# Up runs with the activations stationary, and chunks of u, m and h turned by VectorE and through memory

## What is computed

```
xn = rmsnorm(x);  proj = xn @ w_in
y_mla = mla_branch(proj) @ w_mla_branch;  y_fox = fox_branch(proj) @ w_fox_branch
h  = x + (g_mla * y_mla + g_fox * y_fox) @ w_out        # m is the bracket
hn = rmsnorm(h, mlp_norm)
u  = square(relu(hn @ w_up))                            # 2048 -> 8192
h  = h + u @ w_down                                     # 8192 -> 2048
out = rmsnorm(h, final_norm)
```

## Time and profile before

| | |
|---|---|
| median of three executions | 1311.14 us (1311.02 to 1311.55) |
| the profiled execution, its own time | 1311.39 us |
| its span in the profile | 1309.6 us |
| mean granted clock of TensorE | 0.998 |
| PE busy | 99% of the span |
| DVE / ACT / POOL busy | 57% / 47% / 2% |
| moved by DMA | 251.36 MB, mean 192 GB/s |

### The profile page before, as it was taken

How to read it: one execution, slowest core, us unless ns; L and a number is a source line. 1 busy time by engine, 2 the same in 40 slices (tenths; PEclk the granted TensorE clock), 3 DMA queues, 4 the chain that set the end, 5 groups by cost and what they waited for, 6 DMA issues and landing times.

```text
span 1309.6 us, 15786 instructions
## 1 busy us (share of the span) xinstructions
PE 1300.0 (99%) x6504; PEld 1101.7 (84%) x6504; DVE 751.1 (57%) x803; ACT 609.5 (47%) x744; POOL 22.2 (2%) x20
## 2 busy tenths in 40 slices
PE   9999999999999999999999999999999999999997
PEld 8888888888888888888888888888888888888886
DVE  6676566545666566555666664444456666544543
ACT  6645444545445444454444443333344444444443
POOL 0100000000220000000000000000000000000000
PEclk9999999999999999999999999999999999999999
DMA  8656655556665475566566666666666666666663
GB/s 329 239 186 211 202 165 171 189 168 192 193 193 154 133 241 178 191 189 176 188 189 188 187 190 199 194 193 193 194 185 187 187 187 192 227 191 200 190 194 124
DMA packets 68840, 251.36 MB, mean 192 GB/s; under 512 B 7832, under 2 KB 7840, under 8 KB 68128
## 3 DMA queue, kind: packets, MB, share of 16 engines
q1 hardware_dynamic: 67104, 243.04, 59.8%
q0 software_dynamic: 656, 5.26, 1.1%
q10 hardware_dynamic: 1008, 2.05, 0.4%
HBM read 248.21 MB, written 2.11 MB: 191 GB/s over the span
## 4 chain that ended last, share of the span: by engine, by line
PE 99%; DMA 0%; DVE 0%; ACT 0%; SPq 0%; DVEq 0%; issue 0%; ACTq 0%
PE bank L505 26%; PE bank L585 19%; PE bank L586 19%; PE bank L587 19%; PE bank L510 13%; PE bank L683 1%; PE bank L659 1%; DMA raw<-weights 0%; PE bank L647 0%; PE bank L633 0%; PE bank L631 0%; PE bank L634 0%; PE bank L661 0%; DVE hl L1038 0%; ACT hl L818 0%; PE bank L490 0%
## 5 line engine op out<-in xcount | busy, mean ns | idle before, releaser
L1038 DVE TENSOR_TENSOR hl<-raw,hl 128x1024 fp32r<-128x1024 f32 x455 | 560.5, 1236 | 486.0 <-ACT hl L818 481.1
L818 ACT ACTIVATE hl<-raw 128x1024 fp32r<-128x1024 f32 x455 | 479.5, 1058 | 551.3 <-PE bank L587 383.0
L505 PE MATMUL bank<-hn_hl,hl 128*128 128x512 f32 x1024 | 321.7, 395 | 0.0
L510 PEld LDWEIGHTS bank<-hn_hl,hl 128*128 128x128 f32 x1024 | 192.4, 188 | 45.4
L510 PE MATMUL bank<-hn_hl,hl 128*128 128x256 f32 x1024 | 201.2, 278 | 0.0
L585 PE MATMUL bank<-hl,u_hl 128*128 128x512 f32 x512 | 199.2, 389 | 0.0
L586 PE MATMUL bank<-hl,u_hl 128*128 128x512 f32 x512 | 199.2, 389 | 0.0
L587 PE MATMUL bank<-hl,u_hl 128*128 128x512 f32 x512 | 199.2, 389 | 0.0
L505 PEld LDWEIGHTS bank<-hn_hl,hl 128*128 128x128 f32 x1024 | 156.0, 189 | 0.3
L585 PE MATMUL bank<-hl,x_hl 128*128 128x512 f32 x320 | 125.8, 393 | 0.0
L587 PE MATMUL bank<-hl,x_hl 128*128 128x512 f32 x320 | 124.7, 390 | 0.0
(11 more groups left out here) (180 smaller groups left out, 995.4 us busy)
## 6 DMA issues: line engine op xcount, KB each, us to landing
raw<-weights SPq DMA_DIRECT2D x455, 512.0 KB, 4.2
x_rows<-x_n POOLq DMA_DIRECT2D x2, 1024.0 KB, 10.3
resid<-x_n POOLq DMA_DIRECT2D x1, 2048.0 KB, 8.5
x_in<-x_t SPq DMA_DIRECT2D x3, 512.0 KB, 8.0
cum_k<-cum_rows POOLq DMA_DIRECT2D x1, 1024.0 KB, 7.3
gain_rows<-final_gain SPq DMA_DIRECT2D x1, 1024.0 KB, 4.2
out_n<-final SPq DMA_DIRECT2D x4, 256.0 KB, 2.9
out_n<-final ACTq DMA_DIRECT2D x4, 256.0 KB, 2.8
```

Source lines behind the costliest of these rows:

```text
L505: nc.tensor.matmul(ps, hl[:, slot, 0, col:col + P], x.rearrange("p h t -> p (h t)"), start=first, stop=False)
L510: return nc.tensor.matmul(ps[:, T:], hl[:, slot, 1, col:col + P], x[:, 0], start=False, stop=end)
L818: nc.scalar.activation(hl[:, slot, 0], raw[:, slot], ACT.Copy).then_inc(unit_hi, 1)
L1038: nc.vector.tensor_tensor(hl[:, slot, 1], raw[:, slot], hl[:, slot, 0].bitcast(F32), ALU.subtract).then_inc(unit_split, 1)
```

## The change

Up becomes TOKEN work: `FF_CHUNKS`, eight groups of 8 units for each part, in place of sixteen groups of 4. Its results have tokens on the partitions now, so u has to be turned as well. All chunks of u (16), and the first three chunks each of m and h, 22 in all, are turned in a new way: DVE transposes 32x32 blocks in place of PE's 128x128 (`turn_blocks`, into `blocks`); GpSimd stores `blocks`, 128x1024 float32, to `turn_rows` in memory with one transfer, waits for it, and reads it back with four transfers of 32 partitions each, 4 times 256 elements for a partition, into `turned`. Then ACT and DVE make the high and low part from `turned`. This comes six units (`TURN_UNITS`) after the group's own results are taken. The fourth chunk of m and of h is still turned by PE. The square of the positive part becomes ACT's Relu from PSUM and a multiplication by the bank on DVE. For h the gain is multiplied in by DVE beforehand, in two instructions, in place of ACT's scale.

```diff
@@ the groups @@
-            add(f"up{part}", g, FEATURE, KT // SLABS)
+        for g in range(FF_CHUNKS):
+            add(f"up{part}", g, TOKEN, KT // WIDE_SLABS)
...
-TURN_M = [BY["y_mla", g + 1].u0 + 1 for g in range(3)] + [BY["w_out", 0].u0 + 2]
-TURN_H = [BY["w_out", g + 1].u0 + 3 for g in range(3)] + [BY["up0", 0].u0 + 1]
+TURNED = [("y_mla", g) for g in range(CHUNKS - 1)] + [("w_out", g) for g in range(CHUNKS - 1)]
+TURNED += [(f"up{part}", g) for part in range(MLP_PARTS) for g in range(FF_CHUNKS)]
+TURN_NO = {key: n for n, key in enumerate(TURNED)}
+TURN_UNITS = 6
+TURN_M = BY["w_out", 0].u0 + 2
+TURN_H = BY["up0", 0].u0 + 2
...
+        if (gr.name, gr.g) in TURN_NO:
+            what = {"y_mla": "m turned", "w_out": "h turned"}.get(gr.name, "u turned")
+            after(gr.last + TURN_UNITS, what, gr.g if gr.name[:2] != "up" else gr)
...
@@ GpSimd @@
+            for n in range(len(TURNED)):
+                pool.wait_ge(blocks_turned, n + 1)
+                pool.dma_start(turn_rows[n % 2], blocks[:]).then_inc(blocks_stored, 16)
+                pool.wait_ge(blocks_stored, 16 * (n + 1))
+                if n:
+                    pool.wait_ge(turned_in, 4 * 16 * n)
+                if n >= 2:
+                    pool.wait_ge(turned_split, n - 1)
+                for q in range(4):
+                    pool.dma_start(turned[32 * q:32 * q + 32, n % 2].rearrange("p (a e) -> p a e", a=4),
+                                   turn_rows[n % 2, :, T * q:T * q + T].rearrange("(a p) e -> p a e", a=4)
+                                   ).then_inc(turned_in, 16)
...
@@ TensorE @@
-                token_units(gr, o_mla, last=2)
-                turn_m(g - 1)
-                token_units(gr, o_mla, first=2)
+                token_group(BY["y_mla", g], o_mla)
...
-                token_units(gr, m_hl, last=4)
-                turn_h(g - 1)
-                token_units(gr, m_hl, first=4)
+                token_group(BY["w_out", g], m_hl)
...
-                    else:
-                        feature_units(gr, hn_hl)
+                    else:
+                        token_units(gr, hn_hl)
...
+                def hidden_ready(i, up=up):
+                    pe.wait_ge(turned_split, TURN_NO[up, i // 2] + 1)
...
@@ ScalarE @@
+            def positive_part(gr):
+                act.wait_ge(unit_used, gr.last + 1)
+                act.wait_ge(blocks_turned, TURN_NO[gr.name, gr.g])
+                nc.scalar.activation(full[:], bank[:, gr.pair:gr.pair + 2], ACT.Relu).then_inc(positive, 1)
...
+                n = TURN_NO[gr.name, gr.g]
+                act.wait_ge(turned_in, 4 * 16 * (n + 1))
+                nc.scalar.activation(tiles_of(u_hl, 4 * gr.g, 0), turned_chunk(n), ACT.Copy).then_inc(u_hi, 1)
...
@@ VectorE @@
+            def turn_blocks(name, g, tile):
+                n = TURN_NO[name, g]
+                if n:
+                    dve.wait_ge(blocks_stored, 16 * n)
+                nc.vector.transpose(blocks[:].rearrange("p (q k b j) -> p k b q j", q=4, k=4, b=TB),
+                                    tile.rearrange("p b (k q j) -> p k b q j", k=4, q=4)).then_inc(blocks_turned, 1)
+            def turned_to_lo(n, tile, k0):
+                nc.vector.tensor_tensor(tiles_of(tile, k0, 1), turned_chunk(n), tiles_of(tile, k0, 0).bitcast(F32),
+                                        ALU.subtract).then_inc(turned_split, 1)
...
+                elif gr.name in HIDDEN0:
+                    dve.wait_ge(positive, HIDDEN0[gr.name] + gr.g + 1)
+                    nc.vector.tensor_tensor(full[:], full[:], both, ALU.mult).then_inc(token_out, 1)
+                    dve.wait_ge(token_out, gr.n + 1)
+                    turn_blocks(gr.name, gr.g, full[:])
...
+                    for n_b in range(TB):
+                        ins = nc.vector.tensor_tensor(
+                            turned_chunk(n)[:, :, n_b], turned_chunk(n)[:, :, n_b],
+                            gains.unsqueeze(2).unsqueeze(3).broadcast_to([P, 4, 4, 32]), ALU.mult)
+                    ins.then_inc(h_gained, 1)
```

More of the change, by code:

```diff
@@ L123 @@
 BY = {(gr.name, gr.g): gr for gr in GROUPS}
+RESID0 = {"w_out": 0, "down0": CHUNKS, "down1": 2 * CHUNKS}
 def number_groups():
@@ L164, in make_due @@
                 after(middle, "scored", pair + 1)
[L165 to L171, removed]
+        if (gr.name, gr.g) in TURN_NO:
+            what = {"y_mla": "m turned", "w_out": "h turned"}.get(gr.name, "u turned")
+            after(gr.last + TURN_UNITS, what, gr.g if gr.name[:2] != "up" else gr)
+        if gr.name == "w_out" and gr.g == 0:
+            after(TURN_M, "m turned", CHUNKS - 1)
         elif gr.name == "up0" and gr.g == 0:
-            after(middle - 1, "h turned", 3)
+            after(TURN_H, "h turned", CHUNKS - 1)
         if gr is GROUPS[-1]:
@@ L389, in program @@
         SPLIT0 = {Q_NORM: 0, KV_NORM: KQ}
-        FULL0 = {"up0": 0, "up1": FF_GROUPS}
-        RESID0 = {"w_out": 0, "down0": CHUNKS, "down1": 2 * CHUNKS}
+        HIDDEN0 = {"up0": 0, "up1": FF_CHUNKS}
         FROM_X = ("krff", "fq", "fk")
@@ L952, in take @@
                         nc.scalar.activation(std_col[:, MLP_NORM, 0:1], cst[:, C_EPS:C_EPS + 1], ACT.Sqrt)
-                elif gr.name in ("up0", "up1"):
-                    hidden_hi(gr)
+                elif gr.name in HIDDEN0:
+                    positive_part(gr)
             def m_to_hi(g):
[L957 to L961, removed]
-            def h_to_hi(g):
[L964 to L968, removed]
-                                         scale=gain[:, G_MLP + k:G_MLP + k + 1]).then_inc(h_hi, 1)
+                if g < CHUNKS - 1:
+                    n = TURN_NO["y_mla", g]
+                    act.wait_ge(turned_in, 4 * 16 * (n + 1))
+                    nc.scalar.activation(tiles_of(m_hl, 4 * g, 0), turned_chunk(n), ACT.Copy).then_inc(m_hi, 1)
+                else:
+                    act.wait_ge(m_turned, 1)
+                    nc.scalar.activation(m_hl[:, 4 * g:4 * g + 4, 0],
+                                         bank[:, 6:8].rearrange("p b (f t) -> p (b f) t", f=2),
+                                         ACT.Copy).then_inc(m_hi, 1)
+            def h_to_hi(g):
+                if g < CHUNKS - 1:
+                    act.wait_ge(h_gained, g + 1)
+                    nc.scalar.activation(tiles_of(hn_hl, 4 * g, 0), turned_chunk(TURN_NO["w_out", g]),
+                                         ACT.Copy).then_inc(h_hi, 1)
+                else:
+                    act.wait_ge(h_turned, 1)
+                    for f in range(4):
+                        k = 4 * g + f
+                        nc.scalar.activation(hn_hl[:, k, 0], bank[:, 6 + f // 2, (f % 2) * T:(f % 2) * T + T],
+                                             ACT.Copy, scale=gain[:, G_MLP + k:G_MLP + k + 1]).then_inc(h_hi, 1)
             for u in range(N_UNITS):
@@ new lines, in h_to_lo @@
+            def h_to_lo(g):
+                if g < CHUNKS - 1:
+                    n = TURN_NO["w_out", g]
+                    dve.wait_ge(turned_in, 4 * 16 * (n + 1))
+                    gains = gain[:, G_MLP + 4 * g:G_MLP + 4 * g + 4]
+                    for n_b in range(TB):
[3 more added lines that the diff above has]
+                    ins.then_inc(h_gained, 1)
+                    dve.wait_ge(h_hi, g + 1)
+                    turned_to_lo(n, hn_hl, 4 * g)
+                else:
+                    for f in range(4):
+                        k = 4 * g + f
+                        if f % 2 == 0:
+                            dve.wait_ge(h_hi, g + f + 2)
+                        ins = nc.vector.scalar_tensor_tensor(
+                            hn_hl[:, k, 1], bank[:, 6 + f // 2, (f % 2) * T:(f % 2) * T + T],
+                            gain[:, G_MLP + k:G_MLP + k + 1], hn_hl[:, k, 0].bitcast(F32), ALU.mult, ALU.subtract)
+                    ins.then_inc(h_split, 1)
@@ L1320, in _ @@
                         h_to_lo(g)
+                    elif what == "u turned":
+                        hidden_to_lo(g)
             g = CHUNKS - 1
```

114 lines of the change are left out of this document (54 added, 60 removed).

## The result

The changed kernel takes 1297.79 us (median of 5, 1297.24 to 1297.93) against 1311.24 us for the kernel before on the same chip: a ratio of 0.9896, 95% interval 0.9884 to 0.9907, 13.4 us less. The forecast was 1297.4.

A forecast was written before the change was run, and what follows sets the result against it. PE was taken as full, busy 1300.0 of 1309.6 us. The form's 8.5 and six turns' 5.3 made 13.8 us less, other terms costing 0: 1297.6, or 1297.4 us with the median 0.25 lower; range 1296.2 to 1304.

The forecast's parts named there:

- The form, 8.5 us: In up, TOKEN units need 12 matmuls instead of 16 at equal columns: 0.0663 us less per unit, 8.5 us for 128.
- the rival with so small a gain: In up, fewer matmuls save only 1.3 us, with the turns 6.6 gained: 1304.6 us; chance 0.03.
- The six turns, 5.3 us: Six of eight turns of m and h leave PE, each having cost it 0.88 us: 5.3 us less.
- The new passes beside PE: New ACT and DVE work in up and y_mla runs beside PE, DVE transpose taken as 1.226 us: no gain or loss.
- The trip, X = 10.3: Time from the transpose's end to the last of four reads: 4.3 store, 1.65 issues, 4.3 last landing; cost 0.
- 12.7 forecast: In up, ACT comes to the copy at 17.4 us, the transpose ends at 4.7; X up to 12.7 makes nobody wait.
- 13.2 as the prediction's limit: For the three chunks of h, with the gains of 2 × 0.69 on DVE in the ring, X may be 13.2 us.
- 14.4 as the limit of X at this place: M's chunk 2, used by unit 4 of w_out at 22.6 us, is PE's own tightest need: X may be 14.4.
- The price of being late: If the cover is gone, each of some 19 turns costs its excess over about 14.6 us.
- Its ring, X + 7.2 in a period of 21.8: In up, trip, copy, difference, two low parts, multiply and transpose, X + 7.2 us, must fit 8 × 2.72 = 21.8.
- 14.6: Largest X in us that fits up's period of 21.8 with the other pieces of 7.2.
- A rival with 0.07: The trip through memory is too long, X over 14.6, and the kernel is slower: 1343 us at X = 17; chance 0.07.

The follow-up runs named there:

- the half alone: Against the changed kernel, the six turns of m and h go back to PE, up stays TOKEN work: 1302.87 us, ratio 0.9934 to the kernel before.
- The split product: Changed kernel with one 512-column product in up issued as two of 256 on the same stationary tile: 1306.23 us.
- three kernels: Changed kernel with one spare 512 KB store, two 8 KB stores before each true store, or each transpose done four times: 1361.03, 1383.12 and 1351.40 us.
- an X meant to be 13.2: Changed kernel where GpSimd first stores the same blocks to a spare place and waits, before each true store: 1361.03 us, ratio 1.0393.

## Why the prediction was right

**The form, 8.5 us.** Right: 8.5 by the half alone, and the stage of up1 is 174.08 as forecast (64 x 2.720). It was read from a stage of the same kernel that had the form already, and that is why it held. The split product shows the step behind it: 16.5 ns for each matmul more at the same columns, where the difference of the stages gave 16.6. The 2.5 ns a matmul of the Trainium skill ("TensorE: Matmul & The Clock Gate", section "Wait — 56ns, not 53.3ns?") do not describe these products; the rival with so small a gain (1304.6) is out.

**The six turns, 5.3 us.** Right within what can be told: 4.9 by the times, 5.5 by the two stages. The whole gain was 13.4 against 13.8 summed.

**The new passes beside PE.** Right in size: 1.245 us for the transpose (1.226 taken), 1.21 to 1.22 for the others, 1.01 and 1.05 on ACT. They cost PE nothing.

**The trip, X = 10.3.** Too low, also in up. One turn of up0, the transpose on DVE, the store and the reads on POOL, and the last read as a DMA issue:

```profile
638.73 1.25 DVE L1231 STREAM_TRANSPOSE blocks<-full 128x1024 f32<-128x1024 f32 x1
```

```profile
640.26 0.56 POOL L487 DMA_DIRECT2D turn_rows<-blocks  x1 [16.15 <-DVE blocks L1231]
643.79 2.18 POOL L494 DMA_DIRECT2D turned<-turn_rows  x4 [2.97 <-DMA turn_rows<-blocks]
```

```profile
turned<-turn_rows POOLq DMA_DIRECT2D x1, 128.0 KB, 6.1
```

The store goes out 0.3 us behind the transpose, the first read 3.53 later, the last 1.63 after that, and it lands in 6.1: X = 11.5. Over the 16 turns of up it is 9.7 to 14.2, 11.2 in the median. The store was shorter than the 4.3 taken. The term that was mis-sized is the last read: 4.3 taken, 5.6 in the median of up, for it lands later than the 4.5 that is the median of all four reads. For h X is 13.1, 12.9 and 11.9, with 13.2 as the prediction's limit. In up the conclusion held, since ACT comes to the copy only 12.6 us behind the transpose (12.7 forecast); it waited for `u_hl` once, 1.6 us, at the end of up1. For m the trip was longer: from the ends of the three transposes to ACT's copies it is 12.0, 13.2 and 13.4 us. There, as for h, the conclusion, no wait of PE, held by little, which is luck as much as account. The last of them on DVE, on ACT and on PE, where 514.41 is the first matmul of the unit that needs it:

```profile
496.76 1.25 DVE L1231 STREAM_TRANSPOSE blocks<-gate 128x1024 f32<-128x1024 f32 x1
...
512.51 1.23 DVE L1235 TENSOR_TENSOR m_hl<-turned,m_hl 128x1024 fp32r<-128x1024 f32 x1 [1.86 <-ACT m_hl L990]
```

```profile
511.42 1.06 ACT L990 ACTIVATE m_hl<-turned 128x1024 fp32r<-128x1024 f32 x1 [2.03 <-DMA turned<-turn_rows]
```

```profile
514.41 0.39 PE L617 MATMUL bank<-hl,m_hl 128*128 128x512 f32 x1
```

The difference ends at 513.74, 0.7 us ahead of PE. The prediction had 14.4 as the limit of X at this place; 13.4 was used.

**The price of being late** was the weak step, and the result didn't test it. Its ring, X + 7.2 in a period of 21.8, was right to 0.2 us in three kernels. But it took X as given, and too low. X grows when the trip, or its true store, starts later: in the median of up to 17.6, 18.2 and 13.0 in the three kernels, where the changed kernel's 11.2 with the planned delay gives 14.9, 15.0 and 11.2. Beside it stand fetches of weights in bursts. That ACT is held up doesn't lengthen it by itself: with TURN_UNITS 2, where ACT waits in every turn, X is 10.0 in the median of up. And the stalls of PE cost clock as well. So at an X meant to be 13.2 the kernel lost 63 us where I had 0, and the real room in up, in front of a loss, is 14.6 - 11.2 = 3.4 us, less than the 3.7 that one more store takes. A rival with 0.07 was nearer than it looked. That the fetches lengthen the store is what the traces show side by side; that nothing else does was not tested.

## What to carry to other kernels

Where PE is full, read what a form of work costs from a stage that already has it, from first matmul to first matmul; with float32 in three products here, each matmul more at the same number of columns costs some 16 ns, so few wide ones win. Work taken off a full PE is a gain of its whole length only as long as its way round fits the lead of the other engines; draw that way as a ring with everything in it, and compare it with the period. Take for its length the landing of the last transfer, not the median of all of them. And don't spend the room that such a sum shows: the trip through memory got longer in each kernel here in which it slipped, while the late engines asked for their own transfers all at once.

## What the hardware showed that I had not expected

A DVE transpose of 128x1024 float32 in 32x32 blocks, with four-dimensional views on both sides, takes 1.245 us, hardly more than a sum of two tiles (1.226). A store of 8 KB by GpSimd, waited for, took 3.2 us in the median here beside the weights (1.7 to 5.5), where one had taken 1.6; one of 512 KB took the same 3.2 in the changed kernel. And a quarter more through the DMA engines, 238 GB/s in up0 where it was 191, left the weights' landing where it was, at 4.2 us against 4.3.
